# Cached latents read from a copy that the host has transposed, instead of being transposed on the chip

## What is computed

```python
past_c = cache_kv_latent[l][page_table].reshape(Bd, past_len, KV_LORA)   # 8 x 2048 x 128
past_r = cache_k_rope[l][page_table].reshape(Bd, past_len, A_ROPE)       # 8 x 2048 x 32
q_lat  = einsum('bqhd,chd->bqhc', q_nope, w_uk)
s_past = (einsum('bqhc,bkc->bhqk', q_lat, past_c)
          + einsum('bqhr,bkr->bhqk', q_rope, past_r)) * scale
p      = softmax(concatenate([s_past, s_new], axis=-1), axis=-1)
o_lat  = einsum('bhqk,bkc->bqhc', p[..., :P], past_c) + ...
```

## Time and profile before

| | us |
|---|---|
| median of 3 runs | 2083.25 |
| lowest and highest of them | 2082.23, 2085.16 |
| the profiled execution, its time | 2083.96 |
| its span in the trace | 2082.2 |
| PE busy in the span | 2057.7 |
| DVE, ACT, POOL busy | 1530.5, 1284.7, 119.8 |

### The profile page before, as it was taken

One profiled execution on the slowest core, in us unless ns is written; L12 is line 12 of the kernel. 1 busy time (PEld: TensorE's weight loads), 2 busy tenths in 40 slices (PEclk: granted clock), 3 DMA queues, 4 the chain that ended last, 5 costly groups with the idle time before them and its releaser, 6 DMA issues.

```text
span 2082.2 us, 40614 instructions
## 1 busy us (share of the span) xinstructions
PE 2057.7 (99%) x15542; PEld 1795.5 (86%) x15542; DVE 1530.5 (74%) x3491; ACT 1284.7 (62%) x2535; POOL 119.8 (6%) x138
## 2 busy tenths in 40 slices
PE   8999999999999999999999999999999999999998
PEld 6776799999999888788887758999999998887886
DVE  5854589868899776666577446999688997765766
ACT  5464445658888665565564544556688876655654
POOL 2200010000000010100022000000000001101000
PEclk9999999999999999999999999999999999999999
DMA  9443437776666898898763552577766668988876
GB/s 315 150 154 137 163 130 259 243 259 212 221 214 217 280 316 286 302 324 274 242 226 141 169 182 103 184 254 249 246 221 215 218 211 306 312 282 289 267 263 218
DMA packets 137376, 481.76 MB, mean 231 GB/s; under 512 B 25666, under 2 KB 42082, under 8 KB 130768
## 3 DMA queue, kind: packets, MB, share of 16 engines
q1 hardware_dynamic: 124640, 438.45, 62.5%
q0 software_dynamic: 10496, 40.42, 5.5%
q10 hardware_dynamic: 2048, 0.30, 0.1%
HBM read 475.83 MB, written 104.21 MB: 279 GB/s over the span
## 4 chain that ended last, share of the span: by engine, by line
PE 98%; DVE 1%; ACT 1%; issue 0%; DMA 0%; DVEq 0%; ACTq 0%
PE ps L1187 35%; PE ps L1234 33%; PE ps L828 4%; PE ps L868 4%; PE ps L912 3%; PE ps L1199 3%; PE ps L1150 2%; PE ps L920 2%; PE ps L1158 1%; PE ps L1154 1%; PE ps L877 1%; PE ps L1009 1%; PE ps L1173 1%; PE ps L1012 1%; PE ps L971 1%; PE ps L1025 1%
## 5 line engine op out<-in xcount | busy, mean ns | idle before, releaser
L2141 DVE TENSOR_TENSOR parts<-region,parts 128x1024 fp32r<-128x1024 f32 x512 | 625.9, 1223 | 302.7 <-ACT parts L1486 300.3
L1187 PE MATMUL ps<-tokens_hi,parts 128*128 128x256 f32 x4096 | 760.5, 284 | 0.0
L1486 ACT CAST parts<-region 128x1024 fp32r<-128x1024 f32 x512 | 538.9, 1052 | 272.0 <-PE ps L1234 201.8
L1234 PE MATMUL ps<-parts,parts_hw 128*128 128x512 f32 x3072 | 700.0, 389 | 0.1
L1234 PEld LDWEIGHTS ps<-parts,parts_hw 128*128 128x128 f32 x3072 | 575.6, 188 | 126.6 <-DVE parts_hw L2191 6.9
L1187 PEld LDWEIGHTS ps<-tokens_hi,parts 128*128 128x128 f32 x4096 | 636.6, 188 | 1.0 <-issue 0.5
L1187 PE MATMUL ps<-parts_hw,parts 128*128 128x256 f32 x2048 | 573.7, 280 | 0.0
L1187 PEld LDWEIGHTS ps<-parts_hw,parts 128*128 128x128 f32 x2048 | 386.5, 189 | 0.0
L1532 ACT ACTIVATE big<-ps 128x256 f32<-128x256 f32 (+31 forms) x252 | 131.8, 523 | 146.8 <-PE ps L1187 146.7
L1520 ACT CAST parts_hw<-big 128x256 fp32r<-128x256 f32 x256 | 170.8, 667 | 0.7 <-DVE big L2202 0.7
L1513 ACT ACTIVATE region<-region 128x128 f16<-128x128 f16 x512 | 169.4, 437 | 0.0
(11 more groups left out here) (314 smaller groups left out, 2159.3 us busy)
## 6 DMA issues: line engine op xcount, KB each, us to landing
region<-in_peer_uT SPq DMA_DIRECT2D x256, 512.0 KB, 4.1
region<-in_peer_v SPq DMA_DIRECT2D x256, 512.0 KB, 4.7
out<-in_state_win_k SPq DMA_DIRECT2D x112, 384.0 KB
out<-in_state_win_v SPq DMA_DIRECT2D x112, 384.0 KB
big<-in_window_keysT SPq DMA_DIRECT2D x16, 576.0 KB, 4.0
big<-in_state_win_v SPq DMA_DIRECT2D x48, 192.0 KB, 4.1
region<-in_w_out SPq DMA_DIRECT2D x4, 2048.0 KB, 8.0
big<-in_peer_wq SPq DMA_DIRECT2D x4, 2048.0 KB, 13.9
```

The lines of the kernel that those rows point to most:

```text
L1187: mm = pe.matmul(ps[:, j % ZB, 0:SEQ], a, hp[b][:, c, :], start=(c == 0 and n == 0), stop=(c == KD - 1 and n == 2))
L1234: mm = pe.matmul(ps[:, 2 * half + t, :], w_t[a][:, 128 * t:128 * t + 128], v_t[b][:, 512 * half:512 * half + 512], start=(j == 0 and n == ...
L1486: act.copy(hi_t[n % HIGHS], rows_t[n % ROWS]).then_inc(high[l], 1)
L2141: dve.tensor_tensor(lo_t[n % ROWS], rows_t[n % ROWS], hi_t[n % HIGHS], ALU.subtract).then_inc(low[l], 1)
```

## The change

The host hands over a second copy of the latent cache, cache_latentT, in which each page of 128 tokens by 128 channels is transposed (and its tokens put in the order in which the kernel groups them). The 16 turns cT and the four copies on ACT of each sample are gone; score_past reads the turned pages directly. A turned page is a block of 128 rows of 512 bytes, so that it cannot come with one row per partition for a whole sample: each of the 16 pages of a sample is a DMA of its own, 64 KB. For samples 0, 1, 4, 6 (BY_POOL) GpSimd gathers them with an indirect DMA for each page; for samples 2, 3, 5, 7 (BY_SYNC) SyncE reads the page's number from SBUF into a register and issues a plain DMA from it. The latents as they lie are still loaded for the second use, by GpSimd; both copies need room, so places and waits are new.

```diff
+BY_POOL = (0, 1, 4, 6)
+BY_SYNC = (2, 3, 5, 7)
...
+                def load_turned(b):
+                    for g in range(NPG):
+                        page = sp.value_load(pages[8 * g:8 * g + 1, b:b + 1], min_val=0, max_val=n_phys - 1)
+                        src = A["cache_latentT"][bass.ds(l * n_phys + page, 1)].rearrange("o c t -> (o c) t")
+                        sp.dma_start(turned_at[b][:, PAGE * g:PAGE * g + PAGE], src).then_inc(row_ld[l][BY_SYNC.index(b)], 16)
                 sp.wait_ge(product[now[0]], W_LAST[4])
                 sp.dma_start(ukT, L("w_ukT", l)).then_inc(uq_ld, 16)
+                load_turned(2)
...
                 load_kw(1)
                 load_kw(2)
+                load_turned(3)
+                sp.wait_ge(product[now[0]], NUM["SC", 0] + 1)
+                load_kw(3)
+                sp.wait_ge(product[now[0]], NUM["SC", 1] + 1)
+                load_kw(4)
+                load_kw(5)
+                sp.wait_ge(product[now[0]], NUM["SC", 2] + 1)
+                load_turned(5)
                 sp.wait_ge(product[now[0]], NUM["ol", 0] + 1)
-                load_kw(3)
-                sp.wait_ge(product[now[0]], NUM["ol", 1] + 1)
-                load_kw(4)
+                load_kw(6)
                 sp.wait_ge(product[now[0]], NUM["ws", 0] + 1)
                 load_kw(7)
-                for b in range(4):
+                sp.wait_ge(product[now[0]], NUM["SC", 4] + 1)
+                load_turned(7)
+                for b in (0, 1, 2, 3, 7):
                     load_vw(b)
...
+                def gather_turned(b):
+                    for g in range(NPG):
+                        j = BY_POOL.index(b) * NPG + g
+                        row = bass.IndirectOffsetOnAxis(ap=pidxT[:, j:j + 1].bitcast(U32), axis=0)
+                        pool.indirect_dma_start(turned_at[b][:, PAGE * g:PAGE * g + PAGE], None,
+                                                A["cache_latentT"].rearrange("n c t -> (n c) t"), row).then_inc(erow_u_ld[b], 16)
-                for b in range(4):
+                for b in range(2):
                     load_past(b, "cache_kv_latent", past_ld)
...
+                gather_turned(0)
+                gather_turned(1)
...
-                for b in range(4, NB):
-                    load_past(b, "cache_kv_latent", pastb_ld)
+                for b in (2, 3):
+                    load_past(b, "cache_kv_latent", erow_v_ld[b])
...
                 pool.nop().then_inc(stored, 1)
+                gather_turned(4)
                 wait_moved(pool, "rT", 3)
                 for b in range(4, NB):
                     load_past(b, "cache_k_rope", pastr_ld)
+                pool.wait_ge(product[now[0]], NUM["SC", 3] + 1)
+                load_past(4, "cache_kv_latent", erow_v_ld[4])
+                pool.wait_ge(product[now[0]], NUM["ol", 2] + 1)
+                gather_turned(6)
+                pool.wait_ge(product[now[0]], NUM["ol", 3] + 1)
+                load_past(5, "cache_kv_latent", erow_v_ld[5])
+                pool.wait_ge(product[now[0]], NUM["SC", 5] + 1)
+                load_past(6, "cache_kv_latent", erow_v_ld[6])
+                pool.wait_ge(product[now[0]], NUM["ol", 4] + 1)
+                load_past(7, "cache_kv_latent", erow_v_ld[7])
...
                 def turn_past(b):
-                    for g in range(4):
-                        turn("cT", b, g, parts=[(past_of[b][:, 4 * g + i, :], 128, 128, 128 * i) for i in range(4)])
                     if b == 4:
                         pe.wait_ge(pastr_ld, l * (16 * 4) + 16 * 4)
                     turn("rT", b, parts=[(pastr[:, b % 4, 4 * g:4 * g + 4, :].rearrange("p g c -> p (g c)"), 128, 128, 128 * g) for g in range(4)])
...
                     o = begin("SC", b)
+                    if b in BY_POOL:
+                        pe.wait_ge(erow_u_ld[b], l * (16 * NPG + 16) + 16 * NPG)
+                    else:
+                        pe.wait_ge(row_ld[l][BY_SYNC.index(b)], 16 * NPG)
                     for g in range(4):
-                        pe.matmul(o[32 * g:32 * g + 32, :], qlS[:, b, :], cT[:, g, :], start=True, stop=False, skip_group_check=True)
+                        pe.matmul(o[32 * g:32 * g + 32, :], qlS[:, b, :], pastT_of[b][:, 4 * g:4 * g + 4], start=True, stop=False, skip_group_check=True)
```

More of the change, by code:

```diff
@@ L111, in job_plan @@
             b = PAST_STEP.index(s)
-            jobs += [(("cT", b, g), "A") for g in range(4)] + [(("rT", b), "A")]
+            jobs.append((("rT", b), "A"))
         if 1 <= s <= 2 * NH:
@@ L457, in program @@
         w_mul = sem("late_weights_multiplied")
-        row_ld = [[ctx.enter_context(nc.semaphore(f"u_or_v_loaded{k}_{i}")) for k in range(ROWS)] for i in range(DEPTH)]
+        row_ld = [[ctx.enter_context(nc.semaphore(f"turned_latents_then_u_or_v{k}_{i}")) for k in range(ROWS)] for i in range(DEPTH)]
         h_high = sem("tokens_high")
@@ L1255, in _ @@
                             o_y = begin("gy")
-                        pe.wait_ge(erow_v_ld[b - 1], l * 16 + 16)
-                        pe.wait_ge(erow_v_ld[b], l * 16 + 16)
+                        for r in (b - 1, b):
+                            pe.wait_ge(erow_v_ld[r], (l * 32 + 32) if r >= 2 else (l * 16 + 16))
                         for half in range(2):
@@ L1395, in _ @@
                         b = PAST_STEP.index(s)
-                        for g in range(4):
-                            o = read("cT", b, g)
-                            if b >= 1 and g == 0:
-                                act.wait_ge(product[now[0]], NUM["SC", b - 1] + 1)
-                            act.copy(cT[:, g, :], o[:, 0:512]).then_inc(moved_a[now[0]], 1)
                         o = read("rT", b)
+                        if b >= 1:
+                            act.wait_ge(product[now[0]], NUM["SC", b - 1] + 1)
                         act.copy(rT.rearrange("p g k -> p (g k)"), o[:, 0:512]).then_inc(moved_a[now[0]], 1)
@@ L1668, in _ @@
                     n_rows = A["cache_kv_latent"].shape[1] * 8
+                    step(dve.tensor_scalar(pidxT[:, :], pidxT[:, :], float(n_phys * LAT), None, ALU.add))
+                    settle()
                     dve.tensor_scalar(pidx[:, :], pidx[:, :], float(n_rows), None, ALU.add).then_inc(rows_ready, 1)
```

52 lines of the change are left out of this document (30 added, 22 removed).

## The result

The changed kernel took 2210.4 us (median of 4 runs, 2209.4 to 2211.8) beside 2082.7 us of the kernel before (median of 4, 2080.4 to 2085.2): ratio 1.0609, 95% interval 1.0596 to 1.0622. The forecast was 2126 us, range 2085 to 2165. The sign was right, the size was not: +127.7 us in place of +43.

A forecast was written before the change was run, and what follows sets the result against it. TensorE, busy 99% of the span, was taken as the bound. Per layer 28.5 + 5.2 - 14.4 + 2.3 = +21.6 us, over two layers +43.2 on 2083.96, less 0.7: 2126 us, range 2085 to 2165.

The forecast's parts named there:

- work taken from TensorE is gained in full, unless something else then comes late: TensorE, busy 99% of the span: removing the turns cT gains 1.80 us a sample, 14.4 us per layer.
- TensorE wants them for rT of sample 4 ... that is 124.4: Attention, layer 0: TensorE needs the rope keys at 133.37 less five samples' turns (9.0), that is 124.4 us.
- the wait of 28.5 us for the rope keys: Attention, each layer: rope keys of samples 4 to 7 land at 152.9, wanted at 124.4, so TensorE waits 28.5 us.
- the 5.2 at sample 6: Before SC of sample 6, each layer: its page gathers come late and TensorE waits 5.2 us more.
- lower clock: TensorE after the long wait: slower clock, charged 2.3 us once a layer.
- the store wait that lost its cover: GpSimd waits 9.8 us for its stores to land, formerly hidden under a wait for ACT ending at 119.95.
- the five terms of GpSimd's queue: GpSimd from 50.5: gathers 51.5, stores and latents 11.1, store wait 9.8, gathers 20.8, rope gathers and landing 5.2 + 4.0; ends 152.9.
- the 1.3 that I took: SyncE's time per turned page, between 0.5 and 2.5 us; its 12 us delay stays hidden, binding only above 1.64.
- Cheap gathers (1): Rival: GpSimd's gathers cost towards 0.54 us each, no waits, the whole 28.8 us gained, 2054 us; chance 0.10.
- The floor (2): Rival: every gather 1.25 us, rope keys land in 3.0; first wait 8.4 to 15.2 us, total 2080 to 2094; chance 0.12.
- SyncE (3): Rival: SyncE's page loads bind; at 1.8 us a page 2147 us, at 2.5 us a page 2237; chance 0.15.
- GpSimd starved by VectorE (4): Rival: VectorE's arithmetic slows the first 32 gathers to 1.9 or 2.43 us each, 2145 or 2178 us; chance 0.13.

The follow-up runs named there:

- after_again: The changed kernel word for word, run again on another occasion: 2118.84 us beside 2075.94 for the kernel before, ratio 1.0202.
- lists: The kernel before plus six groups of 16 or 32 idle back-to-back GpSimd gathers, index columns in turn or one column; no gap in any group, no total time given.
- pauses: The kernel before plus groups of idle GpSimd gathers, most with memsets, waits or small DMAs between, two back to back; its one execution took 2088.14 us.

## Why the prediction was wrong, and what of it was right

On the record the failing step is "work taken from TensorE is gained in full, unless something else then comes late": the prediction priced TensorE's stages beside GpSimd's new work at their old length, and so put at nothing, without a reason, what a run of gathers does to an engine that waits for none of them. It asked only who waits for GpSimd's data. That cost 99.5 us of gaps and most of the 55.1 us of slow work: busy time was 2084.0 us, and 2040.0 in after_again, the same kernel without gaps. The sentence "TensorE wants them for rT of sample 4 ... that is 124.4" fell with it: TensorE came there after 165, and the wait of 28.5 us for the rope keys, with the 5.2 at sample 6, did not occur at all.

On the occasions without gaps the same kernel cost +42.9 and +40.7 us, where the sum said +43.2. There the steps can be read one by one. TensorE's waits and GpSimd's timeline in after_again:

```profile
PE ps L863 <- DMA big<-in_cache_k_rope,pidx: 34.6, 2, 17.5
PE ps L1044 <- DMA region<-in_cache_latentT,pidxT: 7.3, 2, 3.7
PE ps L1092 <- DMA big<-in_state_win_v: 4.9, 8, 0.7
PE ps L1044 <- DMA region<-in_cache_latentT: 2.6, 2, 1.5
```

```profile
48.92 0.94 POOL L761 DMA_INDIRECT big<-in_cache_latentT,pidxT  x1 [0.30 <-issue]
...
115.72 1.08 POOL L761 DMA_INDIRECT region<-in_cache_latentT,pidxT  x1 [7.97 <-DMA out<-in_state_conv]
...
135.95 0.94 POOL L754 DMA_INDIRECT big<-in_cache_k_rope,pidx  x1 [0.30 <-issue]
```

| step, layer 0 | predicted | measured (after_again) |
|---|---|---|
| 32 page gathers | 51.5 | 97.04 - 48.92 = 48.1, two of them over 3.5 |
| stores and two latent gathers | 11.1 | 107.75 - 97.04 = 10.7 |
| wait for the stores | 9.8 | 8.0 |
| 16 page gathers of sample 4 | 20.8 | 135.95 - 115.72 = 20.2 |
| four rope gathers, and landing | 5.2 + 4.0 | 143.40 - 135.95 = 7.5 |
| rope keys landed | 152.9 | 143.4 |
| TensorE wants them | 124.4 | 125.9 |
| wait for them | 28.5 | 17.5 |
| second wait, SC of sample 6 | 5.2 | 3.7 |
| waits for SyncE's pages and window values | 0 | 1.5 + 2.5 |
| lower clock | 2.3 | 10.6 by windows, 13.1 by busy time |

**Right** (without gaps): the place, the order and the nature of both waits, and the store wait that lost its cover. **Mis-sized:** each of the five terms of GpSimd's queue was 0.4 to 3.4 us too long and its start 1.6 too late, all in one direction, 9.5 us together; and the clock was too cheap. I had charged it once, for the long wait. In fact the clock dipped in four stretches that lie behind waits:

```profile
115.00:125.90 10.90, 10.02 (x138) 0.84 0.73 242
125.90:143.40 17.50, 0.00 (x0) 0.62 0.66 197
143.40:160.00 16.60, 16.60 (x219) 0.89 0.35 116
160.00:180.00 20.00, 15.91 (x227) 0.91 0.69 238
...
200.00:220.00 20.00, 20.00 (x77) 0.74 0.57 211
```

An estimate of the work lost is the share missing times the length: 0.16 x 10.9 + 0.11 x 16.6 + 0.09 x 20 + 0.26 x 20 = 10.6 us, where lists, which is the kernel before in these stages, has 1.00 throughout. The two errors went against each other, so the total of +43 was right in part by luck. Layer by layer it was not even: layer 0 cost 25.1 us more than in lists (GpSimd's first memset of layer 1 at 1063.47 against 1038.35) and layer 1 13.6 (span 2112.4 against 2073.7, less that), for a predicted 21.6 each. (That is 38.7 us in all: the profiled execution of after_again, 2114.27 us, is the fastest of four, and the median is 4.6 above it.) Of layer 0's 25.1 the table gives 17.5 + 3.7 + 4.0 + 10.6 - 14.4 = 21.4, and 1.4 more are there by GpSimd's first memset of the program (21.13 against 19.72). Most of the other 2.3 is slow work that the windows miss: up to the memset of layer 1 TensorE is busy for 1029.26 us, in lists for 1030.57, so with 14.4 us of turns gone the rest took 13.1 longer. In layer 1 it is busy for 1010.75 against 1021.65, only 3.5 longer. Its idle time grew by 24.5 us, much as in layer 0 (26.4). So nearly the same waits cost 13.1 us of clock in one layer and 3.5 in the other; why is open.

**SyncE** took 18.56 / 16 = 1.16 us a page for sample 2 in the changed kernel and 17.48 / 16 = 1.09 in after_again, under the 1.3 that I took and under the 1.64 at which it binds. Beside gathers, with gaps, it took 28.05 / 16 = 1.75 for sample 3. The Trainium skill's floor of about 600 ns for a register load ("DMA: Bandwidth & Descriptors", section "Latency and other measured facts") made an estimate of about 1.1 us a page. The sum agrees with that estimate, the part does not: the register loads (TENSOR_LOAD) of after_again last 0.275 us in the median, 0.263 at the least. **The product** with the pages in pieces of eight took 1.06 us, as before: nothing, as taken.

**The rivals.** Cheap gathers (1): no, they stayed at 1.24 us or more. The floor (2): for the first wait its upper end, 15.2 us, was nearer to the 17.5 than my 28.5, but its total was not, since it left out the clock. SyncE (3): no. GpSimd starved by VectorE (4): in part; in after_again two of the 32 gathers took 4.38 and 3.65 us, 4.69 and 3.97 to the next start, where one of 5.04 was taken, and the others followed each other in 1.24 to 1.65. The right rival, TensorE starved by GpSimd, was missing, and the range could not hold it.

## What to carry to other kernels

A run of indirect gathers back to back on GpSimd can make gaps in TensorE's and SyncE's work, on some occasions and not on others, even where nobody waits for the gathers; short "issue" gaps beside existing gathers are the sign. How long the run must be depends on what TensorE does: beside products of 256 columns 16 gathers did it and 8 did not, beside shorter ones 4 did. Break such runs up: half a microsecond of a memset or a plain DMA between two was enough in pauses. Or give page-number loads to SyncE, which left TensorE no gaps and 3.7 us of waits for window values. And when a change makes TensorE wait, look at the clock behind every wait: the charge for one long wait was too low in both layers.

## What was not expected of the hardware

- With gaps, TensorE went on for 63, 64 and 63 matmuls of 256 columns, 7.2 to 7.3 us, before the first one, but 61 shorter ones in 3.4 us in the kernel before; then, in the changed kernel, single products came at multiples of about 0.70 us (76.82, 80.32, 83.12, 85.22: 3.50, 2.80, 2.10 apart).
- With gaps, SyncE too was held up: 16 pages beside the gathers of sample 4 took 28.05 us (26.33 in layer 1). In after_again, without gaps, 16 pages beside the same gathers took 17.32.
- The kernel before itself is 5 to 8 us faster on occasions without gaps (2075.9 to 2077.8 against 2082.7 to 2083.6), more than its 3 us of visible gaps.
- A gather takes GpSimd the same 1.25 us from start to start with 64-byte as with 512-byte rows, and 1.17 (0.86 + 0.30) with a quarter of the rows; what it does to TensorE is as little a matter of what it moves.
